# Stick-breaking attention: running sums over softplus values split into a rounded part and a remainder

## The reference, cut to what matters

```python
z = jnp.einsum('bhqd,bhkd->bhqk', qb, kb).astype(jnp.float32) * scale
strict = s_idx < t_idx
log_keep = jnp.where(strict, jax.nn.log_sigmoid(-z), 0.0)
tail = lax.cumsum(log_keep, axis=3, reverse=True) - log_keep
log_w = jax.nn.log_sigmoid(z) + tail
w = jnp.where(strict, jnp.exp(log_w), 0.0)
outs.append(jnp.einsum('bhqk,bhkd->bhqd', w.astype(v.dtype), vb))
```

## Time and profile before

| | |
|---|---|
| median of 3 runs | 2173.36 us (2165.53 to 2173.94) |
| the profiled execution, its own time | 2173.69 us |
| its span in the trace | 2171.9 us |
| TensorE matmul busy | 2017.6 us, 93% |
| VectorE, ScalarE, GpSimd busy | 1065.1, 739.1, 782.7 us |
| stick-breaking stage in the trace | from 96.3 to 204.2 us |

### The profile page before, as it was taken

The page is one execution under the profiler, slowest core; times in us unless marked ns, Lnnn a source line. Parts: engine busy times, 40 slices in busy tenths (PEclk is TensorE's granted clock), DMA queues, the critical chain, the costliest instruction groups (busy, mean ns, idle before and its releaser), DMA issues.

```text
span 2171.9 us, 24975 instructions
## 1 busy us (share of the span) xinstructions
PE 2017.6 (93%) x9426; PEld 1616.4 (74%) x9426; DVE 1065.1 (49%) x1314; ACT 739.1 (34%) x889; POOL 782.7 (36%) x225
## 2 busy tenths in 40 slices
PE   6999978989899999978799999999998899999999
PEld 4855946867677888766477888887788777888887
DVE  5133142135885176285658632652978536431430
ACT  5243123333323233432544222233325544222221
POOL 3201302434343543431033434434349343434433
PEclk9999957999999999989999999999999999999999
DMA  4200201234353454230044524543132122223222
GB/s 165 81 1 20 88 20 39 77 96 153 139 191 100 162 193 137 94 123 20 1 145 145 193 99 170 192 143 103 62 110 81 40 97 78 97 80 107 97 78 103
DMA packets 45928, 223.82 MB, mean 103 GB/s; under 512 B 4880, under 2 KB 9104, under 8 KB 31008
## 3 DMA queue, kind: packets, MB, share of 16 engines
q1 hardware_dynamic: 45424, 221.00, 29.4%
q10 hardware_dynamic: 432, 1.84, 0.2%
HBM read 220.68 MB, written 2.13 MB: 103 GB/s over the span
## 4 chain that ended last, share of the span: by engine, by line
issue 50%; PE 29%; POOL 11%; DVE 6%; ACT 3%; POOLq 0%; DMA 0%; DVEq 0%; SPq 0%; ACTq 0%
PE pairs L458 15%; POOL wl L1789 11%; PE pairs L482 5%; PE pairs L473 4%; PE pairs L501 1%; DVE arena L1683 1%; DVE arena L401 1%; PE aux L761 1%; PE aux L747 1%; DVE arena L1667 1%; ACT wh L427 1%; PE aux L750 1%; PE aux L740 1%; DVE arena L819 0%; DVE arena L812 0%
## 5 line engine op out<-in xcount | busy, mean ns | idle before, releaser
L1789 POOL TENSOR_TENSOR wl<-raw,wh 128x2048 fp32r<-128x2048 f32 (+2 forms) x173 | 721.8, 4174 | 1369.3 <-ACT wh L427 1369.3
L458 PE MATMUL pairs<-xh,wh 128*128 128x512 f32 x1368 | 543.8, 397 | 48.6 <-DVE zl L670 21.6
L458 PE MATMUL pairs<-xh,wl 128*128 128x512 f32 x1368 | 537.8, 393 | 0.0
L458 PE MATMUL pairs<-xl,wh 128*128 128x512 f32 x1368 | 537.0, 393 | 0.0
L427 ACT ACTIVATE wh<-raw 128x2048 fp32r<-128x2048 f32 x173 | 330.0, 1908 | 272.6 <-PE pairs L482 150.6
L458 PEld LDWEIGHTS pairs<-xh,wh 128*128 128x128 f32 x1368 | 260.2, 190 | 112.9 <-DVE zl L670 24.6
L458 PEld LDWEIGHTS pairs<-xh,wl 128*128 128x128 f32 x1368 | 260.6, 190 | 55.1 <-issue 1.5
L458 PEld LDWEIGHTS pairs<-xl,wh 128*128 128x128 f32 x1368 | 260.2, 190 | 55.1
L670 DVE TENSOR_TENSOR zl<-arena,zh 128x512 f32 (+1 forms) x66 | 211.1, 3199 | 90.6 <-ACT zh L637 90.6
L482 PE MATMUL pairs<-zh,wh 128*128 128x512 f32 x518 | 204.9, 395 | 14.1 <-POOL wl L1789 14.1
L482 PE MATMUL pairs<-zh,wl 128*128 128x512 f32 x518 | 202.9, 392 | 0.0
(11 more groups left out here) (278 smaller groups left out, 2700.8 us busy)
## 6 DMA issues: line engine op xcount, KB each, us to landing
raw<-in_w SPq DMA_DIRECT2D x115, 1024.0 KB, 5.0
arena<-in_ada SPq DMA_DIRECT2D x96, 512.0 KB, 4.4
raw<-in_w SPq DMA_DIRECT2D x48, 704.0 KB, 4.1
raw<-in_w SPq DMA_DIRECT2D x10, 512.0 KB, 3.5
arena<-mx_rows SPq DMA_DIRECT2D x16, 256.0 KB, 3.6
h<-in_xT SPq DMA_DIRECT2D x4, 512.0 KB, 8.3
outT<-h SPq DMA_DIRECT2D x8, 256.0 KB, 4.4
arena<-in_pool ACTq DMA_DIRECT2D x1, 1024.0 KB, 8.2
```

The lines of the kernel that those rows point to most:

```text
L458: mm = p.matmul(pairs[:, 2 * slot + m, :], w[:, slot, at:at + P], src[part][:, k, :], start=(k == 0 and w is wh and part == 0), stop=(k == ...
L1789: g.tensor_tensor(wl[:, slot, 0:w], raw[:, slot, 0:w], wh[:, slot, 0:w].bitcast(F), ALU.subtract).then_inc(lo_done, 1)
```

## The change

The sums now run over two float32r tiles in place of one float32 tile. After mult(n), ScalarE copies sp to a rounded tile (hi), and GpSimd subtracts that from sp, which gives a rounded remainder (lo). `tri(n)` runs its ladder of matmuls twice in float32r, over hi and over lo, each behind its own semaphore. The four constant matrices are copied once to float32r. The hi and lo tiles are double buffered by head in rows 4 to 10 of `zh` and `zl`, which are free at that time; the float32 sp tile is double buffered by step. GpSimd makes the remainder of the first `g_q` weight chunk before the stage, as it did, and the stage's loop stands between it and the rest. In the linear-attention stage that follows (`gla_*`), seven semaphores are folded into one counter with the same order of waits.

```diff
-                p.wait_ge(b_sp, n + 1)
-                p.matmul(aux[:, n % 3, 0:w], cm("ntri"), SB_SP[i], start=False, stop=False,
-                         skip_group_check=True)
-                for j in range(i + 1, TB):
-                    p.matmul(aux[:, n % 3, (j - i) * P:w], cm("nones"), SB_SP[j], start=False, stop=False,
+                if n == 0:
+                    p.wait_ge(b_cst, 4)
+                for part, ready in ((SP_HI, b_hi), (SP_LO, b_lo)):
+                    p.wait_ge(ready, n + 1)
+                    p.matmul(aux[:, n % 3, 0:w], SB_CST[:, 0:P], part[hd % 2][i], start=False, stop=False,
                              skip_group_check=True)
-                p.matmul(aux[:, n % 3, 0:P], cm("ident"), cm("neg_strict"), start=False, stop=True,
+                    for j in range(i + 1, TB):
+                        p.matmul(aux[:, n % 3, (j - i) * P:w], SB_CST[:, P:2 * P], part[hd % 2][j], start=False,
+                                 stop=False, skip_group_check=True)
+                p.matmul(aux[:, n % 3, 0:P], SB_CST[:, 2 * P:3 * P], SB_CST[:, 3 * P:4 * P], start=False, stop=True,
                          skip_group_check=True).then_inc(b_tri, 1)
...
         def sb_act(a):
+            a.wait_ge(consts, 16)
+            for i, name in enumerate(("ntri", "nones", "ident", "neg_strict")):
+                a.activation(SB_CST[:, i * P:(i + 1) * P], cm(name), ACT.Copy).then_inc(b_cst, 1)
             a.preload_act_table_set("natural_log_exp_and_others")
...
                 if n:
                     weights(n - 1)
+                hd, i = n // TB, TB - 1 - n % TB
+                a.wait_ge(b_sp, n + 1)
+                a.activation(SP_HI[hd % 2][i], SB_SP[:, n % 2, 0:w], ACT.Copy).then_inc(b_hi, 1)
                 if n % (2 * TB) == 1 and n > 1:
                     out_hi(n // (2 * TB) - 1)
...
+        def sb_gpsimd(g):
+            for n in range(SB_N):
+                hd, i = n // TB, TB - 1 - n % TB
+                g.wait_ge(b_hi, n + 1)
+                g.tensor_tensor(SP_LO[hd % 2][i], SB_SP[:, n % 2, 0:T - P * i], SP_HI[hd % 2][i].bitcast(F),
+                                ALU.subtract).then_inc(b_lo, 1)
...
                 v.wait_ge(b_ln, n + 1)
-                if n % TB == 0 and n:
-                    v.wait_ge(b_tri, n)
-                elif n:
-                    if n >= TB:
-                        v.wait_ge(b_tri, n - n % TB)
-                v.tensor_tensor(SB_SP[i], aux[:, n % 3, 0:w], el, ALU.max).then_inc(b_max, 1)
+                if n >= 2:
+                    v.wait_ge(b_lo, n - 1)
+                if n >= 2 * TB:
+                    v.wait_ge(b_tri, n - n % TB - TB)
+                sp = SB_SP[:, n % 2, 0:w]
+                v.tensor_tensor(sp, aux[:, n % 3, 0:w], el, ALU.max).then_inc(b_max, 1)
...
+                if stage == "g_q":
+                    continue
...
+                if stage == "sb_v":
+                    body(C0["g_q"], C0["g_q"] % 2, 0)
+                    sb_gpsimd(g)
```

More of the change, by code:

```diff
@@ L722, in build, with sp_parts @@
         SB_W = arena[:, 14:16, :]
-        SB_SPA = arena[:, 16:19, :].rearrange("p a b -> p (a b)")
+        SB_SP = arena[:, 16:18, :]
         sp_at = [0, 512, 896, 1152]
-        SB_SP = [SB_SPA[:, sp_at[i]:sp_at[i] + T - P * i] for i in range(TB)]
+        def sp_parts(z):
+            flat_ = [z[:, at:at + 3, :].rearrange("p a b -> p (a b)") for at in (4, 8)]
+            return [[f_[:, sp_at[i]:sp_at[i] + T - P * i] for i in range(TB)] for f_ in flat_]
+        SP_HI, SP_LO = sp_parts(zh), sp_parts(zl)
+        SB_CST = zh[:, 7, :]
+        b_cst, b_hi, b_lo = sem("b_cst"), sem("b_hi"), sem("b_lo")
         b_qk, b_cap, b_exp, b_ln = sem("b_qk"), sem("b_cap"), sem("b_exp"), sem("b_ln")
@@ L813, in sb_dve @@
                 v.wait_ge(b_ln, n + 1)
-                if n % TB == 0 and n:
-                    v.wait_ge(b_tri, n)
-                elif n:
-                    if n >= TB:
-                        v.wait_ge(b_tri, n - n % TB)
-                v.tensor_tensor(SB_SP[i], aux[:, n % 3, 0:w], el, ALU.max).then_inc(b_max, 1)
+                if n >= 2:
[4 more added lines that the diff above has]
+                v.tensor_tensor(sp, aux[:, n % 3, 0:w], el, ALU.max).then_inc(b_max, 1)
                 v.wait_ge(b_max, n + 1)
-                v.tensor_tensor(SB_SP[i][:, 0:P], SB_SP[i][:, 0:P], cm("keep_strict"), ALU.mult).then_inc(b_sp, 1)
+                v.tensor_tensor(sp[:, 0:P], sp[:, 0:P], cm("keep_strict"), ALU.mult).then_inc(b_sp, 1)
                 if n % (2 * TB) == 1 and n > 1:
@@ L839, in build @@
         gla_in = sem("gla_in")
-        g_pre, g_nx, g_cap, g_e, g_l = sem("g_pre"), sem("g_nx"), sem("g_cap"), sem("g_e"), sem("g_l")
-        g_sp, g_cum, g_eqk, g_diff, g_ee = sem("g_sp"), sem("g_cum"), sem("g_eqk"), sem("g_diff"), sem("g_ee")
-        g_ki, g_ke, g_tr, g_kt = sem("g_ki"), sem("g_ke"), sem("g_tr"), sem("g_kt")
+        g_pre, g_e, g_l, g_eqk, g_ee = sem("g_pre"), sem("g_e"), sem("g_l"), sem("g_eqk"), sem("g_ee")
+        g_dec = sem("g_dec")
+        G_DEC = {"nx": 2, "cap": 3, "sp": 4, "cum": 6, "diff": 7, "ke": 8, "ki": 9}
+        g_tr, g_kt = sem("g_tr"), sem("g_kt")
         g_att, g_at, g_ds, g_st, g_o = sem("g_att"), sem("g_at"), sem("g_ds"), sem("g_st"), sem("g_o")
@@ L906, in gla_act @@
             a.preload_act_table_set("natural_log_exp_and_others")
-            a.wait_ge(g_cap, 1)
+            a.wait_ge(g_dec, G_DEC["cap"])
             a.activation(G_EL, G_EL, ACT.Exp).then_inc(g_e, 1)
@@ L938, in gla_dve @@
                 v.tensor_scalar(G_NX[:, j, :], aux[:, j, :], -1.0, pc("b_alpha", j), ALU.mult, ALU.subtract
-                                ).then_inc(g_nx, 1)
-            v.wait_ge(g_nx, 2)
-            v.tensor_scalar(G_EL, G_NX, SP_CAP, None, ALU.min).then_inc(g_cap, 1)
+                                ).then_inc(g_dec, 1)
+            v.wait_ge(g_dec, G_DEC["nx"])
+            v.tensor_scalar(G_EL, G_NX, SP_CAP, None, ALU.min).then_inc(g_dec, 1)
             v.wait_ge(g_l, 1)
-            v.tensor_tensor(G_NX, G_NX, G_EL, ALU.max).then_inc(g_sp, 1)
-            v.wait_ge(g_sp, 1)
+            v.tensor_tensor(G_NX, G_NX, G_EL, ALU.max).then_inc(g_dec, 1)
+            v.wait_ge(g_dec, G_DEC["sp"])
             for j in range(2):
                 v.tensor_tensor_scan(G_CUM[:, j, :], G_RESET, G_NX[:, j, :], 0.0, ALU.mult, ALU.add
-                                     ).then_inc(g_cum, 1)
-            v.wait_ge(g_cum, 2)
+                                     ).then_inc(g_dec, 1)
+            v.wait_ge(g_dec, G_DEC["cum"])
             cum = G_CUM.rearrange("p j (n c) -> p (j n) c", c=GLA_C)
@@ L951, in gla_dve @@
                             cum[:, :, GLA_C - 1:GLA_C].to_broadcast([P, 2 * GN, GLA_C]), cum, ALU.subtract
-                            ).then_inc(g_diff, 1)
+                            ).then_inc(g_dec, 1)
             v.wait_ge(g_ee, 1)
-            v.tensor_tensor(G_EE, GK, G_EE, ALU.mult).then_inc(g_ke, 1)
+            v.tensor_tensor(G_EE, GK, G_EE, ALU.mult).then_inc(g_dec, 1)
             v.wait_ge(g_eqk, 2)
             v.tensor_tensor(GQ, GQ, G_EQ, ALU.mult)
-            v.wait_ge(g_ke, 1)
-            v.tensor_tensor(GK, GK, G_EK, ALU.mult).then_inc(g_ki, 1)
+            v.wait_ge(g_dec, G_DEC["ke"])
+            v.tensor_tensor(GK, GK, G_EK, ALU.mult).then_inc(g_dec, 1)
             v.wait_ge(g_tr, 2)
             v.tensor_copy(G_KT, aux[:, 2:4, :]).then_inc(g_kt, 2)
-            v.wait_ge(g_ki, 1)
+            v.wait_ge(g_dec, G_DEC["ki"])
             for hd in range(GLA_H):
```

8 lines of the change are left out of this document (4 added, 4 removed).

## The result

| | median | runs | profiled execution | its span | mean granted clock |
|---|---|---|---|---|---|
| before | 2174.25 us (2165.49 to 2190.74) | 15 | 2173.69 us | 2171.9 us | 0.962 |
| after | 2197.96 us (2195.27 to 2204.45) | 15 | 2202.15 us | 2200.4 us | 0.943 |

The changed kernel takes 1.0108 times as long (95% interval 1.0088 to 1.0129), 23.7 us more by the medians. The two profiled executions differ by 28.5 us. Predicted were 2215 us and a range of 2179 to 2221.

The account below looks back on a forecast made before the run. TensorE's own work and a chain through the other engines together bound the 107.9 us stage. Changed: eight heads at 0.50 146.2, filling and draining 3.1, less 1.3: 148; next stage 1.8; 41.9 more, 2215 us, range 2179 to 2221.

Parts of the forecast that it names:

- The case forecast as the likeliest: Changed stage: clock at 0.50 from 100 us to its end, stage 148 us, kernel 2215 us; chance 0.55.
- the clock flipping: Rival, changed stage: clock rises at a 512-wide group now and then, falls at a pair's end; about 2197 us; chance 0.17.
- the clock stays down to the end of the stage: Changed stage: split 512-wide ladders, half-array pv and qk, and waits keep the clock at 0.50; eight heads 146.2 us.
- At 0.50 a head: Changed stage, TensorE the bound: qk and pv 8.5, tri 6.4, twelve group starts 3.2, wait 0.2: 18.3 us.
- the 42: Whole kernel, likeliest case: 41.9 us more than before, including about 1.8 us lost by the next stage's dense matmuls.
- the lower end of the prediction, 2203: Lower end of the likeliest case: 128-wide matmuls don't double at the low clock, 11 us.
- 12.95 and 13.98 us: Changed stage's chain per head at full clock, plain and ending a pair, in place of 12.21 and 12.69 us.
- the queues' 110.6 us: Changed stage's length at full clock, worked through the instruction queues; 102.6 us for the kernel before.
- Each microsecond at the low clock: Changed stage, clock flipping: each microsecond at 0.50 costs 0.26 us.
- Prices: Changed stage's new operations: hi copy on ScalarE 0.63 us at 512; lo on GpSimd 0.48 to 1.30 us by width.
- The double buffering at nothing: Softplus stage: max's wait for the head before, 20.2 us over 7 times, goes, but wasn't in the chain; no gain.
- mult and the shared port: VectorE's mult against GpSimd's lo: only the 128 step's mult loses about 0.25 us, off the chain; upper bound 3.6 a head.

Follow-up runs that it names:

- two dummies: The changed kernel with two dummy float32r matmuls of 512 columns, result unused, behind the first ladder of each step: 2187.56 us, 1.0052 to before.
- With four: The changed kernel with four dummy float32r matmuls of 512 columns, result unused, behind the first ladder of each step: 2191.64 us, 1.0079 to before.
- the reordered kernel: The changed kernel with six PSUM banks for scores, qk four steps ahead, weights two steps behind: 2158.63 us, 0.9927 to before.
- the two float32 kernels: The kernel before with two sets of softplus arrays, 2186.29 us; the same plus six banks, qk four ahead, weights two behind, 2175.53 us.
- the reordered float32 kernel: The kernel before with two sets of softplus arrays, six banks, qk four steps ahead, weights two behind: 2175.53 us, 1.0000 to before.

## Why the prediction was right, and where it was not

The time lies in the range, and the direction was right, for the two reasons given: a longer chain and a lower clock. The case forecast as the likeliest did not happen. The rival did that had the clock flipping (0.17, about 2197 us), and the measured 2198 is in its place. That it fits to 1 us is luck: 2197 stood for half of the stage at the lower clock, where 66% were, and 7.5 us of the profiled difference come from behind the stage, which no sum had.

- **The step that failed** is "I take it that the clock stays down to the end of the stage". The clock rose in six 512-wide steps and fell again after five of them. The argument had two halves. That TensorE's sparser load keeps the clock low more of the time was right (85 us at 0.50 against about 14). That the lo wait inside the 512-wide tri group, and pv and qk on half of the array around it, would keep it from rising was wrong: all six rises came while pv and qk streamed, behind that group. What decides between a rise and none stays open. The kernel with the remainders at VectorE, which differs by one engine and some tenths of a microsecond, came near the forecast case (139.3 us).
- **At 0.50 a head** was to take 18.3 us: 17.63 measured. TensorE as the bound there was right (busy for 42.20 of the 44.00 us from 164 to 208); eight times 0.67 is 5 us of the 42. Most of it lies in the tri groups: from 172.18 to 189.82 us their four take 6.9 us to the start of the pv behind them, where the sum gives 7.5 (6.4, and 1.1 for their share of the group starts). I had doubled every 128-wide matmul. In a wide group at 0.50 the mask matmul begins 0.11 us after the 128-wide one ahead of it, as at full clock; the lower end of the prediction, 2203, had allowed for that:

```profile
171.73 0.31 PE L759 MATMUL aux<-zl,zh 128*128 128x128 f32 x1
171.84 0.41 PE L761 MATMUL aux<-zh 128*128 128x128 f32 x1
```

- **At full clock** 12.95 and 13.98 us, average 13.46. With two dummies 13.00: the plain head is right. The head with a pair's end took 14.5, but at a mean clock of 0.88; at 0.22 us for each of its 3.5 low us it would be about 13.7 at full clock, an estimate, so the 13.98 was a little too long. With four, all heads took 14.06 against 14.2. Taking the queues' 110.6 us for the stage at full clock, 8 us of the stage's 21.0 are the chain; the rest, 13, is what the clock costs beyond the 5 to 6 us that it cost before. This split is an estimate, since the changed kernel never ran at a held clock without dummies.
- **Each microsecond at the low clock** was to cost 0.26; 128.9 - 110.6 = 18.3 over 85 us is 0.22.
- **Prices**: lo 1.275 for 1.30 at 512, 0.455 for 0.48 at 128; hi 0.627 for 0.63. The remainders at a held clock cost 0.85 us a head, expected 0.8.
- **The double buffering at nothing**: right in the stage, shown by the float32 kernel that has it alone.
- **mult and the shared port**: 0.25 us on the 128 step was expected, mult's longest is 293 ns. In the reordered kernel, where GpSimd's remainders lie elsewhere in the step, it does happen: mean 360 ns, longest 607. Seven of its 32 mults start about 0.45 us before a subtraction ends and take 0.60 to 0.61 us in place of 0.29; one of them is shown below. The Trainium skill, "SBUF — State Buffer", section "Who interferes with whom", calls the port an exclusive lock; that agrees with the reordered kernel. In the changed one three mults meet the last 0.08 to 0.09 us of a remainder and none is held up.

```profile
151.88 1.28 POOL L827 TENSOR_TENSOR zl<-arena,zh 128x512 fp32r<-128x512 f32 x1 [3.85 <-ACT zh L816]
...
152.71 0.61 DVE L849 TENSOR_TENSOR arena<-arena,cst 128x128 f32<-128x128 f32 x1
```

- **Not foreseen**: 7.5 us behind the stage. Two pieces of it, 3.1 and 2.1 us, come in the same two sizes in other runs: the two float32 kernels and the one with remainders at VectorE have only the second, all the others have both. So the second, 2.0 to 2.1 us, is in every trace but that of the kernel before, and may belong to that one execution as much as to any edit. The folded semaphores were never tried alone; the 1.4 us in the stretch that holds them stand against 1.3 in the reordered float32 kernel, which doesn't fold them. What sets these pieces stays open.

## What to carry to other kernels

Before work is taken off TensorE, see which engine's chain ends last: here the rounded sums are lighter by 2 us a head and, in the schedule as it stood, lengthened the serial chain by 1 us (both by the prediction's sums), and they let the clock fall; only with scores four steps ahead did they pay. A stage that leaves TensorE waiting pays twice, so keep it fed, with real work from further ahead or, at a stage's start, with a few dummy matmuls. A stage is to be judged by its own length as well as by the kernel's time: the float32 reordering saved 11.8 us in its stage, and the up projections gave 10.0 of it back.

## What the hardware showed that I had not expected

**The clock fell six times and rose six times in one stage of 129 us**, and a lighter load can cost what it saves: with lo left out the mean clock fell from 0.67 to 0.54, and the stage kept all but 3.0 us; with lo kept and 64 dummy matmuls added it rose from 0.67 to 0.90. The length of a wait alone doesn't tell when the clock falls: in the 7 us before the fall at 120.0 us TensorE never stood idle for more than 0.4 us, and the reordered float32 kernel waited 0.74 us at 100.7 and stayed at full clock. What exactly decides a rise can't be read from these runs.

**The up projections have three lengths.** The stretch that holds them lies between 439 and 1006 us before. In all twelve traces it takes 560 to 562, 567 to 568 or 577 us, and the mean of VectorE's L658 there is 929, 2032 or 3330 ns, one to one. The middle one is the kernel before, the changed one, and two with dummies. The long one is the two float32 kernels with two buffers; the other six have the short one. How long TensorE waits goes with it and makes up 5.1 of the 10 us from the middle to the long one and 3.8 of the 6 from the short to the middle one; the rest was not followed. Here before, the reordered float32 kernel, and the reordered one with the change (total, times, longest):

```profile
PE pairs L458 <- DVE zl L670: 13.2, 7, 9.4
```

```profile
PE pairs L458 <- DVE zl L670: 18.3, 14, 9.4
```

```profile
PE pairs L458 <- DVE zl L670: 9.4, 1, 9.4
```

The reordered float32 kernel's timeline at the place shows the mechanism:

```profile
802.25 4.90 POOL L1793 TENSOR_TENSOR wl<-raw,wh 128x2048 fp32r<-128x2048 f32 x1 [6.95 <-ACT wh L427]
...
802.61 4.82 DVE L658 TENSOR_SCALAR arena<-arena,par 128x512 f32<-128x512 f32 x1
```

L658's durations in this kernel (min/median/max ns), and the same place in the kernel before:

```profile
L658 DVE TENSOR_SCALAR arena<-arena,par x22: 541/4806/4829, 552.2 to 860.6; 128x512 f32<-128x512 f32 x22
```

```profile
798.58 5.14 POOL L1789 TENSOR_TENSOR wl<-raw,wh 128x2048 fp32r<-128x2048 f32 x1 [5.73 <-ACT wh L427]
...
801.56 2.72 DVE L670 TENSOR_TENSOR zl<-arena,zh 128x512 f32 x1 [0.93 <-ACT zh L637]
```

L658 takes 0.55 us when alone. In the reordered float32 kernel it starts 0.36 us after GpSimd's subtraction and ends 0.28 us after it: it stood still for nearly all that time. The Trainium skill, "SBUF — State Buffer", section "Who interferes with whom", states this lock, and names tensor_scalar among the operations that can meet it; the trace agrees. Before, in the same place, it is L670 that meets the subtraction, and takes 2.72 us in place of 0.69. L658 is at the head of VectorE's chain for a chunk and L670 at its end, so which of them is caught decides how late the chunk is. No line of these stages was edited in any run; what differs is when they begin and what came before. That the relative phase of GpSimd's weight subtraction and VectorE's chain picks the length is what the rows suggest; what sets the phase was not tried.
